# Projections of a streaming encoder: one pass over the channel tiles for both token groups, instead of one pass for each

## The chip, the cores and the metric
The kernel runs on one core of one Trainium2 chip. The metric is device time in microseconds (us) of one execution; a profile is taken of one execution, and its times count from the start of its span.

## The reference
Two layers of a hybrid streaming encoder are computed for 512 prompt frames, 16 meta tokens and 32 new frames of a sample stream, 560 tokens of 1024 channels in all. What matters here is that nearly all of the arithmetic is dense projections:

```python
h = _rmsnorm(x, p['g_pre_mix'])
... = _split_cols(h @ p['w_in'])          # queries, keys, values, three branch gates
y = (g[..., 0, :] * (oa @ p['w_up_a']) + g[..., 1, :] * (ob @ p['w_up_b'])
     + g[..., 2, :] * (oc @ p['w_up_c']))
x = x + _rmsnorm(y @ p['w_out'], p['g_post_mix'])
f = jnp.square(jax.nn.relu(_rmsnorm(x, p['g_pre_mlp']) @ p['w_ff1'])) @ p['w_ff2']
```

Branch A is latent attention, B is sliding-window attention, C is a gated linear recurrence (GLA).

## The kernel before
**Units.** Tokens lie along the free axis, channels on the 128 partitions. The weights of a layer are cut into 151 units of 128 x 1024 values, each with a kind and a number: `kralr`, `cq`, `ck`, `cv`, `cg`, `ckv` (branch C and latents), `qr`, `qn`, `qb`, `kb`, `vb`, `gate_a/b/c`, `up_a/b/c`, `out`, `ff1`, `ff2`. A unit makes 128 output channels from 8 channel tiles, or (`up_a`, `up_b`) two sets of 128 output channels from 4 channel tiles each.

**Token groups.** The 560 tokens are two halves of 280 (`H[0]`, `H[1]`), because one PSUM bank takes one half. Each float32 operand is held as a rounded high part and a low part (`hi_w`, `lo_w` of the weights, `hi_x`, `lo_x` of the tokens), and a product is three matmuls, called records here: high by high, low weight by high, high weight by low. A half of a unit is therefore 24 records into one bank, a whole unit 48.

**Order.** A plan written by hand (`layer_plan`, `lap`) gives the order of steps, the same for every engine. A step `("dense", u)` is a whole unit, `("half", u, hf)` one half of it; between them stand the steps of the three branches (`gla`, `att`, `prep_a`, `b`). `dense_unit` issues a unit on TensorE. Near the turn from one layer part to the next, halves are issued apart; there are 117 whole units a layer, and one of them (`out` 0) has a branch of its own in `dense_unit`.

**Banks.** Six PSUM banks serve the units, given out at build time to the half whose turn it is, least recently used first, out of a set that depends on the unit:

```python
b = 5 if key in guests else min(SIX if wide else FOUR if ... else THREE if ... else TWO, key=lambda c: bank_free[c])
```

`out`, `ff1` and `ff2` take from six banks. Units from `qb` 1 to the last `up_b` take from three. Nearly all others, those of the GLA and attention stretches, take from two, because attention and the recurrence hold the rest. `wait_bank` makes TensorE wait until the bank's previous half has been evacuated.

**Evacuation.** ScalarE (ACT) evacuates `ck`, `cg`, `vb`, `out`, `ff1`; VectorE (DVE) the rest, half 0 and then half 1, in the order of the plan. A gate's half goes through both: on ACT an absolute value (L1386), an exponential (L1387) and a logarithm (L1388), then on DVE the step that frees the bank (L1785), then on ACT a last exponential (L1390); only then does ACT turn to the other half. GpSimd (POOL) computes the low parts of weights and scales attention probabilities.

Of the kernel before, what the change touches and what calls it, by code (L numbers as in the profile page):

```python
# [88 lines left out]
def outs_of(kind):  # L89

    return (2, 4) if kind in ("up_a", "up_b") else (1, KD)
# [51 lines left out]
def build(nc, io, known):  # L143
    st = Steps(known)
    ctx = ExitStack()
    with ctx:
        def sem(name):
            return ctx.enter_context(nc.semaphore(name))
# [159 lines left out]
        pe_done, act_done, dve_done, pool_done = (sem(n) for n in ("pe_done", "act_done", "dve_done", "pool_done"))  # L308
# [63 lines left out]
        for i, m in enumerate((1, 2, 4, 8, 16)):  # L372
            a = 2 * 128 + i * (META + DEC) // 2
# [13 lines left out]
        def program(block):  # L387
            H = (slice(0, HALF), slice(HALF, T))

            def A(e, n, layer=None):  # L390
                return st.at(e, n, st.layer if layer is None else layer)
# [5 lines left out]
            def source(kind, n):  # L397
                if kind == "up_c":
                    return "oc"
                if kind == "up_a":  # L400
                    return "oa"
                if kind == "up_b":
                    return "ob"
                if kind == "out":
                    return "y"
                if kind == "ff1":
                    return "h2"
                if kind == "ff2":
                    return "hid%d" % (n // 8 % 2)
                return "h"  # L410

            def ready_names(kind, n, k):

                s = source(kind, n)
                if s == "ob":
                    return ("act", "ob hi 4"), ("pool", "ob lo 4")
                if s.startswith("hid"):
                    g = n // 8
                    return ("act", f"hid hi {8 * g + k}"), ("pool", f"hid lo {8 * g + k}")
                lo = y_engine_of_lo(k) if s == "y" else "dve" if s == "oc" else "pool"  # L420
                return ("act", f"{s} hi {k}"), (lo, f"{s} lo {k}")

            def y_engine_of_lo(k):
                return "dve" if k >= 6 else "pool"

            def evac_engine(kind):
                return "act" if kind in ("ck", "cg", "out", "ff1", "vb") else "dve"
# [241 lines left out]
            for l_ in range(DEPTH):  # L669
                for u in range(NU):  # L670
                    kind, n = UNITS[u]
# [9 lines left out]
            for l_, step in plan:  # L681
# [15 lines left out]
                while begun and split and most:  # L697
                    key = split[0]
# [17 lines left out]
            for i, key in enumerate(halves):  # L716
                l_, u, o, hf = key
                kind = UNITS[u][0]
                wide = kind in ("out", "ff1", "ff2") or u in V_NEXT
                b = 5 if key in guests else min(SIX if wide else FOUR if UIDX["qn", 2] <= u <= UIDX["up_c", 0] else THREE if UIDX["qb", 1] <= u < UIDX["out", 0] else TWO, key=lambda c: bank_free[c])  # L720
# [10 lines left out]
            def low_split(u):  # L731
                return (dve_done, A("dve", f"w lo {u}")) if (st.layer, u) in on_dve else (pool_done, A("pool", f"w lo {u}"))

            def bank(u, o, hf):
                return bank_of[st.layer, u, o, hf]
# [9 lines left out]
            by_name = {"pe": pe_done, "act": act_done, "dve": dve_done, "pool": pool_done}  # L745
# [133 lines left out]
            def _(pe):  # L879
                first_use = set()  # L880

                def wait_bank(u, o, hf):
                    prev = before[l, u, o, hf]
                    if (l, u, o, hf) in guests:
                        i = guests[l, u, o, hf]
                        pe.wait_ge(dve_done, A("dve", f"b o {i - 1}" if i > 0 else f"a o {len(jobs) - 1}"))
                    if prev is not None:
                        pl, pu, po, ph = prev
                        e = evac_engine(UNITS[pu][0])
                        pe.wait_ge(by_name[e], A(e, f"evac {pu} {po} {ph}", pl))  # L890

                def dense_unit(u, hfs):
                    kind, n = UNITS[u]
                    nout, kt = outs_of(kind)
                    slot = slot_of[l, u]
                    hi_w = whi[slot][:, :].rearrange("p (k m) -> p k m", k=kt)
                    lo_w = wlo[slot][:, :].rearrange("p (k m) -> p k m", k=kt)
                    src = source(kind, n)
                    hi_x, lo_x = moving[src]
                    halved = src in ("h", "h2")  # L900
                    pe.wait_ge(act_done, A("act", f"w hi {u}"))
                    pe.wait_ge(*low_split(u))
                    if kind == "qn" and n == 2:
                        pe.wait_ge(act_done, A("act", f"gla rstd {C_HEADS - 1}"))
                    if kind == "out" and n == 0:
                        pe.wait_ge(dve_done, A("dve", "b o 4"))
                    m = 112 if kind == "kralr" else 128
                    if src == "y" and n == 0:

                        for hf in range(2):  # L910
                            wait_bank(u, 0, hf)
                        for k in range(kt):
                            for e, name in ready_names(kind, n, k):
                                pe.wait_ge(by_name[e], A(e, name))
                            for hf in range(2):
                                for i, (a, b) in enumerate(((hi_w, hi_x), (lo_w, hi_x), (hi_w, lo_x))):
                                    mm = pe.matmul(bank(u, 0, hf)[0:m, :], a[:, k, 0:m], b[:, k, H[hf]],
                                                   start=(k == 0 and i == 0), stop=(k == kt - 1 and i == 2))
                                if k == kt - 1:
                                    mm.then_inc(pe_done, st.done("pe", f"half {u} 0 {hf}"))  # L920
                        st.mark("pe", f"dense {u}")
                        return
                    for o in range(nout):
                        for hf in hfs:
                            wait_bank(u, o, hf)
                            key = (l, src, n // 8 if kind == "ff2" else 0, hf if halved else 0)
                            fresh = key not in first_use
                            first_use.add(key)
                            for k in range(kt):
                                if fresh and halved:  # L930
                                    which, at_l = ("next", l - 1) if src == "h" else ("pre_mlp", l)
                                    pe.wait_ge(act_done, A("act", f"{which} hi {k} {hf}", at_l))
                                    pe.wait_ge(dve_done, A("dve", f"{which} lo {k} {hf}", at_l))
                                elif fresh:
                                    for e, name in ready_names(kind, n, k):
                                        pe.wait_ge(by_name[e], A(e, name))
                                for i, (a, b) in enumerate(((hi_w, hi_x), (lo_w, hi_x), (hi_w, lo_x))):
                                    mm = pe.matmul(bank(u, o, hf)[0:m, :], a[:, k, o * 128:o * 128 + m], b[:, k, H[hf]],  # L938
                                                   start=(k == 0 and i == 0), stop=(k == kt - 1 and i == 2))
                            mm.then_inc(pe_done, st.done("pe", f"half {u} {o} {hf}"))  # L940
                    if hfs[-1] == 1:
                        st.mark("pe", f"dense {u}")
# [376 lines left out]
                for l, step in order:  # L1319
# [22 lines left out]
                    elif step[0] == "att":  # L1342
                        br, j = step[1], step[2]
                        n = len(JOBS[br])
# [1232 lines left out]
```

## Time and profile before

| | us |
|---|---|
| median of 3 runs | 2324.94 (2324.63 to 2325.22) |
| the profiled execution's own time | 2323.95 |
| its span | 2322.2 |
| TensorE matmul busy | 2283.4 (98%) |
| VectorE, ScalarE, GpSimd busy | 915.2, 995.9, 934.7 |

The profiled execution is 1 us under the median, and 1.75 us of its time lie around the span. In the rows below, `PE` is TensorE's matmuls and `PEld` its weight loads; a row of a timeline has the start, the duration, the engine, the line, the operation, the tile written and those read, and in brackets the idle time before it with what ended that. Durations of matmuls overlap: how fast they follow each other is read from their starts. `dense<-` are records into banks 0 and 1, `att<-` records into the other banks.

### The profile page before, as it was taken

What the parts mean: (1) busy time and instruction counts of PE and PEld (TensorE: products, weight loads), DVE (VectorE), ACT (ScalarE), POOL (GpSimd) and SP (SyncE); (2) the same over time, 40 slices, a digit from 0 to 9 for tenths busy, and PEclk for the clock granted to TensorE, in tenths of its full rate; (3) what the DMA queues carried; (4) which work ended last, traced back from release to release, by engine and by line L of the source; (5) the groups of instructions that cost most, each with busy time, mean ns of one, the idle gap of its engine ahead of it and who ended that gap; (6) DMA issues with size and microseconds to landing.
All of it is one profiled execution on the core that took longest, in us unless ns stands there. A gap on an engine that the chain in (4) does not pass through costs nothing.

```text
span 2322.2 us, 41257 instructions
## 1 busy us (share of the span) xinstructions
PE 2283.4 (98%) x17472; PEld 2167.5 (93%) x17472; DVE 915.2 (39%) x1909; ACT 995.9 (43%) x1879; POOL 934.7 (40%) x600
## 2 busy tenths in 40 slices
PE   7999999999999999999999999999999999999997
PEld 7999978889899999999999999788999999999997
DVE  6566555544514401001575664555344153000014
ACT  4444334443555642332344444344345556433412
POOL 2222224444665453544412222144455645545432
PEclk9999999999999999999999999999999999999999
DMA  5121221122124222222321222211212241222222
GB/s 193 54 65 62 84 78 58 55 63 73 63 82 154 69 82 91 83 85 71 118 88 53 72 62 88 68 61 56 72 65 65 82 167 55 83 91 82 89 80 72
DMA packets 59815, 187.89 MB, mean 81 GB/s; under 512 B 8400, under 2 KB 17552, under 8 KB 59120
## 3 DMA queue, kind: packets, MB, share of 16 engines
q1 hardware_dynamic: 51408, 169.28, 23.1%
q10 hardware_dynamic: 8224, 15.97, 1.9%
q8 instruction: 139, 2.28, 0.4%
q14 instruction: 44, 0.36, 0.0%
HBM read 170.99 MB, written 10.89 MB: 78 GB/s over the span
## 4 chain that ended last, share of the span: by engine, by line
PE 92%; DVE 5%; ACT 1%; issue 1%; POOL 0%; DMA 0%; SPq 0%; DVEq 0%; ACTq 0%
PE dense L938 44%; PE att L938 30%; PE att L1013 2%; PE att L1242 1%; PE att L1153 1%; PE att L1090 1%; PE att L1173 1%; PE att L1280 1%; PE dense L967 1%; PE att L1094 1%; PE att L1076 1%; PE att L1315 1%; PE att L1201 1%; PE att L1177 1%; DVE x L1879 1%
## 5 line engine op out<-in xcount | busy, mean ns | idle before, releaser
L2299 POOL TENSOR_TENSOR wlo<-wraw,whi 128x1024 fp32r<-128x1024 f32 x245 | 588.4, 2409 | 596.8 <-ACT whi L1367 596.8
L938 PE MATMUL dense<-h_hi,whi 128*128 128x280 f32 x1888 | 557.4, 295 | 1.2 <-issue 0.9
L938 PE MATMUL dense<-h_lo,whi 128*128 128x280 f32 x1888 | 551.0, 292 | 0.0
L938 PE MATMUL dense<-h_hi,wlo 128*128 128x280 f32 x1888 | 549.9, 291 | 0.0
L1367 ACT ACTIVATE whi<-wraw 128x1024 fp32r<-128x1024 f32 x302 | 315.0, 1050 | 267.9 <-DMA wraw<-in_w 265.2
L938 PEld LDWEIGHTS dense<-h_hi,whi 128*128 128x128 f32 x1888 | 355.6, 188 | 14.5 <-issue 11.1
L938 PEld LDWEIGHTS dense<-h_hi,wlo 128*128 128x128 f32 x1888 | 355.1, 188 | 0.5
L938 PEld LDWEIGHTS dense<-h_lo,whi 128*128 128x128 f32 x1888 | 355.4, 188 | 0.0
L938 PE MATMUL att<-h_hi,whi 128*128 128x280 f32 x1024 | 299.3, 292 | 0.4 <-issue 0.4
L938 PE MATMUL att<-h_lo,whi 128*128 128x280 f32 x1024 | 298.3, 291 | 0.0
L938 PE MATMUL att<-h_hi,wlo 128*128 128x280 f32 x1024 | 297.8, 291 | 0.0
L938 PE MATMUL att<-hid_hi,whi 128*128 128x280 f32 x672 | 196.0, 292 | 0.0
L938 PEld LDWEIGHTS att<-h_hi,whi 128*128 128x128 f32 x1024 | 192.4, 188 | 3.5 <-ACT sig L1390 1.6
L938 PE MATMUL att<-hid_lo,whi 128*128 128x280 f32 x672 | 195.6, 291 | 0.0
L938 PE MATMUL att<-hid_hi,wlo 128*128 128x280 f32 x672 | 195.3, 291 | 0.0
L938 PEld LDWEIGHTS att<-h_hi,wlo 128*128 128x128 f32 x1024 | 192.2, 188 | 0.3
L938 PEld LDWEIGHTS att<-h_lo,whi 128*128 128x128 f32 x1024 | 192.4, 188 | 0.0
L2304 POOL TENSOR_TENSOR hid_lo<-hid_raw,hid_hi 128x560 fp32r<-128x560 f32 (+1 forms) x76 | 93.6, 1231 | 239.0 <-ACT hid_hi L1371 239.0
L2347 POOL TENSOR_TENSOR level<-bcum 128x256 f32<-128x256 f32 (+2 forms) x56 | 42.8, 764 | 262.6 <-DVE bcum L1928 262.6
L938 PEld LDWEIGHTS att<-hid_hi,whi 128*128 128x128 f32 x672 | 126.3, 188 | 0.1
L938 PEld LDWEIGHTS att<-hid_lo,whi 128*128 128x128 f32 x672 | 126.3, 188 | 0.0
L938 PEld LDWEIGHTS att<-hid_hi,wlo 128*128 128x128 f32 x672 | 126.2, 188 | 0.1
(366 smaller groups left out, 4581.2 us busy)
## 6 DMA issues: line engine op xcount, KB each, us to landing
wraw<-in_w SPq DMA_DIRECT2D x302, 512.0 KB, 3.5
x_spill<-x ACTq DMA_DIRECT2D x2, 2240.0 KB, 7.0
x<-x_spill ACTq DMA_DIRECT2D x2, 2240.0 KB, 11.9
k_cat<-k_rope SPq DMA_DIRECT2D x16, 212.0 KB, 3.4
x<-in_x SPq DMA_DIRECT2D x4, 560.0 KB, 6.0
out_y_out<-x SPq DMA_DIRECT2D x4, 560.0 KB, 3.1
out_c_out<-ckv SPq DMA_DIRECT2D x2, 560.0 KB, 5.4
state<-in_state ACTq DMA_DIRECT2D x8, 128.0 KB, 2.1
```

Source lines behind the costliest of these rows:

```text
L938: mm = pe.matmul(bank(u, o, hf)[0:m, :], a[:, k, o * 128:o * 128 + m], b[:, k, H[hf]], start=(k == 0 and i == 0), stop=(k == kt - 1 and i ...
L967: mm = pe.matmul(bank(u, 0, hf)[0:m, :], a[:, k, 0:m], b[:, k, H[hf]], start=(k == 0 and i == 0), stop=(k == KD - 1 and i == 2))
L1013: mm = pe.matmul(ps[0:rows, PAIR_BANK[i], c0:c0 + 64].rearrange("p (g t) -> p g t", t=m), e[:, 128 * sb:128 * sb + rows], late, start=(n_ ...
L1076: mm = pe.matmul(ps[:, bank, 256 * (sb % 2):256 * (sb % 2) + 256], ktok[0:n, sb, :], vtok[0:n, sb, :], start=(sb % 2 == 0), stop=True, ski ...
L1090: pe.matmul(dst, vtok[0:n, sb, 128 * vt:128 * vt + 128], amat[0:n, a:a + n], start=first, stop=(sb == 0), skip_group_check=True)
L1094: mm = pe.matmul(dst, state[:, STATE_IN[sb], 128 * vt:128 * vt + 128], qe[:, a:a + n], start=False, stop=True, skip_group_check=True)
L1153: mm = pe.matmul(ps[0:n, pair + i, 0:512], src[:, k, a:a + n], wuv[:, k, :], start=(k == 0), stop=(k == KL - 1))
L1173: mm = pe.matmul(ps[:, S0 + a, 0:META + 128 * (i + 1)], q_cat[:, h, 128 * i:128 * i + 128], k_cat[:, h, K_META:K_FRAME + 128 * (i + 1)], s ...
L1367: act.activation(whi[slot][:, :], wraw[slot][:, :], ACT.Copy).then_inc(act_done, st.done("act", f"w hi {u}"))
L2299: pool.tensor_tensor(wlo[slot][:, :], wraw[slot][:, :], whi[slot][:, :].bitcast(F32), ALU.subtract).then_inc(pool_done, st.done("pool", f" ...
L2304: pool.tensor_tensor(lo, raw, hi.bitcast(F32), ALU.subtract).then_inc(pool_done, st.done("pool", name))
L2347: pool.tensor_tensor(e_first, ref, b_first, ALU.subtract).then_inc(pool_done, st.done("pool"))
```

## The change
A branch is added to `dense_unit` for calls with both halves. For each set of output channels it first waits for the banks of both halves, then goes through the channel tiles once. For each tile it issues six records: high weight by high half 0 and half 1, high weight by low half 0 and half 1, low weight by high half 0 and half 1. So four records with the same stationary tile stand in a row, then two, and the bank changes at each record. Halves that are issued apart (`("half", ...)`, `("pair", ...)`) and `out` 0 are as before, and so are the bank of each half, the plan and the order on every other engine.

```diff
--- before.py
+++ after.py
@@ -920,6 +920,25 @@
                                     mm.then_inc(pe_done, st.done("pe", f"half {u} 0 {hf}"))
                         st.mark("pe", f"dense {u}")
                         return
+                    if len(hfs) == 2:
+                        for o in range(nout):
+                            for hf in hfs:
+                                wait_bank(u, o, hf)
+                            key = (l, src, n // 8 if kind == "ff2" else 0, 0)
+                            fresh = key not in first_use
+                            first_use.add(key)
+                            for k in range(kt):
+                                if fresh:
+                                    for e, name in ready_names(kind, n, k):
+                                        pe.wait_ge(by_name[e], A(e, name))
+                                for i, (a, b, hf) in enumerate(((hi_w, hi_x, 0), (hi_w, hi_x, 1), (hi_w, lo_x, 0), (hi_w, lo_x, 1),
+                                                                (lo_w, hi_x, 0), (lo_w, hi_x, 1))):
+                                    mm = pe.matmul(bank(u, o, hf)[0:m, :], a[:, k, o * 128:o * 128 + m], b[:, k, H[hf]],
+                                                   start=(k == 0 and i < 2), stop=(k == kt - 1 and i >= 4))
+                                    if k == kt - 1 and i >= 4:
+                                        mm.then_inc(pe_done, st.done("pe", f"half {u} {o} {hf}"))
+                        st.mark("pe", f"dense {u}")
+                        return
                     for o in range(nout):
                         for hf in hfs:
                             wait_bank(u, o, hf)
```

TensorE, inside unit `gate_b` 0 of layer 0, before: the end of half 0 (bank 1, `dense`) and the start of half 1 (bank 4, `att`), where the wait for that bank's evacuation stands.

```order
L938 MATMUL dense<-h_hi,whi_77 128x280
L938 MATMUL dense<-h_hi,wlo_64 128x280
L938 MATMUL dense<-h_lo,whi_77 128x280
L938 MATMUL att<-h_hi,whi_77 128x280 [waits dve_done]
L938 MATMUL att<-h_hi,wlo_64 128x280
L938 MATMUL att<-h_lo,whi_77 128x280
```

TensorE, the end of the same unit and the start of `gate_b` 1 (banks 0 and 1) now.

```order
L936 MATMUL dense<-h_hi,whi_77 128x280
L936 MATMUL att<-h_hi,whi_77 128x280
L936 MATMUL dense<-h_lo,whi_77 128x280
L936 MATMUL att<-h_lo,whi_77 128x280
L936 MATMUL dense<-h_hi,wlo_64 128x280
L936 MATMUL att<-h_hi,wlo_64 128x280
L936 MATMUL dense<-h_hi,whi_75 128x280 [waits dve_done,pool_done,act_done]
```

The two halves end side by side, and the wait for both banks of the next unit stands ahead of its first record.

TensorE, where `gate_b` 1 (banks 0 and 1, here `dense0` and `dense1`) ends and `up_b` 0 begins, before; `up_b` 0 takes banks 4 and 0 for its first output channels.

```order
L938 MATMUL dense1<-h_lo_89,whi0_75 128x280
L938 MATMUL dense1<-h_hi_90,whi0_75 128x280
L938 MATMUL dense1<-h_hi_90,wlo0_62 128x280
L938 MATMUL dense1<-h_lo_89,whi0_75 128x280
L938 MATMUL att<-ob_hi_155,whi1_76 128x280 [waits act_done,dve_done,pool_done]
L938 MATMUL att<-ob_hi_155,wlo1_63 128x280
L938 MATMUL att<-ob_lo_154,whi1_76 128x280
```

The same place now.

```order
L936 MATMUL dense0<-h_hi_90,wlo0_62 128x280
L936 MATMUL dense1<-h_hi_90,wlo0_62 128x280
L936 MATMUL att<-ob_hi_155,whi1_76 128x280 [waits dve_done,act_done,pool_done]
L936 MATMUL dense0<-ob_hi_155,whi1_76 128x280
L936 MATMUL att<-ob_lo_154,whi1_76 128x280
L936 MATMUL dense0<-ob_lo_154,whi1_76 128x280
L936 MATMUL att<-ob_hi_155,wlo1_63 128x280
L936 MATMUL dense0<-ob_hi_155,wlo1_63 128x280
```

Bank 0 was last written 24 records before `up_b` 0 and is needed 12 records into it; now it is written until two records ahead of it and needed at once.

## Rows read from the trace of the kernel before

**Rows 1.** Page: busy us, share of the span, instructions.
```profile
PE 2283.4 (98%) x17472; PEld 2167.5 (93%) x17472; DVE 915.2 (39%) x1909; ACT 995.9 (43%) x1879; POOL 934.7 (40%) x600
```

**Rows 2.** Page: chain that ended last, share of the span by engine.
```profile
PE 92%; DVE 5%; ACT 1%; issue 1%; POOL 0%; DMA 0%; SPq 0%; DVEq 0%; ACTq 0%
```

**Rows 3.** Windows: us, then busy us (count) by engine, granted clock, DMA share, GB/s.
```profile
634.00:709.00 75.00, 75.00 (x585) 74.63 (x583) 13.92 (x33) 43.32 (x83) 47.69 (x28) 1.00 0.28 86
802.00:1123.00 321.00, 321.00 (x2502) 321.00 (x2501) 22.82 (x51) 107.64 (x159) 158.05 (x80) 1.00 0.28 86
```

**Rows 4.** TensorE's waits: who waited for whom, total us, times, longest.
```profile
PE att L981 <- DVE nsum L1856: 15.3, 5, 10.8
...
PE att L1280 <- DVE qb L1816: 1.5, 2, 0.7
```

**Rows 5.** Line L1100: durations of loads and records, two calls with one stationary each time.
```profile
L1100 PEld LDWEIGHTS att<-gsq,const x32: 189/189/190, 120.8 to 1438.1; 128*128 128x128 f32 x32
L1100 PE MATMUL att<-gsq,const x32: 398/398/399, 121.0 to 1438.4; 128*128 128x280 f32 x32
```

**Rows 6.** Timeline, ff1 and ff2 units: start us, us, engine, line, operation.
```profile
833.41 0.41 ACT L1426 ACTIVATE hid_raw<-att 128x280 f32<-128x280 f32 x1 [2.69 <-PE att L938]
...
870.20 0.29 PE L938 MATMUL att<-hid_hi,whi 128*128 128x280 f32 x1
...
870.40 0.45 DVE L1831 COPY facc<-att 128x280 f32<-128x280 f32 x1 [2.62 <-PE att L938]
```

**Rows 7.** Timeline around the end of gate_c 2, all engines.
```profile
375.20 1.02 PE L1177 MATMUL att<-k_cat,q_cat 128*128 128x512 f32 x2
...
375.40 0.40 ACT L1386 ACTIVATE sig<-dense 128x280 f32<-128x280 f32 x1 [0.66 <-PE dense L938]
...
376.85 0.45 DVE L1785 SCALAR_TENSOR_TENSOR sig<-dense,sig 128x280 f32<-128x280 f32 x1 [2.58 <-ACT sig L1388]
...
377.33 0.44 ACT L1390 ACTIVATE sig<-sig 128x280 f32<-128x280 f32 x1 [0.58 <-DVE sig L1785]
...
377.53 0.17 DVE L2112 MEMSET att<- 64x128 f32 x1 [0.24 <-PE att L1178]
...
379.55 0.39 PE L938 MATMUL dense<-oc_hi,whi 128*128 128x280 f32 x1
```

**Rows 8.** Timeline, TensorE after gate_c 1 and after gate_a 1.
```profile
358.29 1.08 PE L1173 MATMUL att<-k_cat,q_cat 128*128 128x272 f32 x4
...
359.86 0.37 PE L938 MATMUL dense<-oc_hi,whi 128*128 128x280 f32 x1
...
500.97 0.29 PE L938 MATMUL dense<-h_lo,whi 128*128 128x280 f32 x1
501.49 1.09 PE L1201 MATMUL att<-const,prob 128*128 128x128 f32 x8 [0.22 <-POOL prob L2373]
...
502.44 0.38 PE L938 MATMUL dense<-h_hi,whi 128*128 128x280 f32 x1
```

**Rows 9.** Timeline: probabilities of attention job 3, and TensorE's use of them.
```profile
384.22 1.95 POOL L2373 TENSOR_TENSOR prob<-prob,stat 128x1056 f32<-128x1056 f32 x1 [3.06 <-DVE stat L2190]
...
387.07 1.09 PE L1201 MATMUL att<-const,prob 128*128 128x128 f32 x8
```

**Rows 10.** Timeline in the preparation of the keys, after gate_c 0.
```profile
334.40 0.17 DVE L2084 COPY k_cat<-att 64x16 f32<-64x16 f32 x1
...
334.62 0.53 PEld L1147 LDWEIGHTS att<-cct,wuk 128*128 128x128 f32 x3 [0.51 <-DVE k_cat L2084]
```

**Rows 11.** Timeline, TensorE between two units of the GLA stretch.
```profile
173.21 1.10 PE L1100 MATMUL att<-gsq,const 128*128 128x280 f32 x4
173.94 0.50 PE L938 MATMUL dense<-h_hi,whi 128*128 128x280 f32 x1
```

**Rows 12.** Windows around one wait in each layer; columns as in rows 3.
```profile
772.00:784.00 12.00, 9.61 (x59) 8.97 (x58) 10.33 (x18) 8.43 (x19) 2.90 (x3) 0.86 0.00 1
1921.00:1933.00 12.00, 9.63 (x72) 8.99 (x70) 10.33 (x18) 8.60 (x20) 2.91 (x3) 1.00 0.01 1
```

## The prediction
> **What bounds the kernel now.** The page comes first: matmuls are busy for 2283.4 us, 98% of the span [rows 1], and 92% of the chain that ended last runs through TensorE [rows 2]. So the question for every edit is whether TensorE's stream of records gets shorter, or gets holes. Next, the windows. In the last projections of a layer (634 to 709 us) and in the MLP (802 to 1123 us) TensorE is busy for the whole stretch; there 2502 records take 321 us, one each 0.128 us [rows 3]. A whole unit of 48 records takes 6.16 us. Then TensorE's waits: the longest group is 15.3 us, and 1.5 us in two places is already the fourth [rows 4]. No group of waits for a bank is in that list. The evacuations are hidden entirely, and what hides them is the order: while a half is evacuated, the other half of the same unit is computed, 24 records or 3.08 us.
>
> **What the change does to the records.** Of 117 whole units a layer 116 take the new branch: 232 units, 11,136 records. None is removed or added. Is a record cheaper when its stationary tile is the one before? The nearest rows are those of L1100, where two calls in a row have the same constant as stationary tile: 32 records, and 32 weight loads of 189 ns [rows 5]. Each record brings its load all the same. So the load of a repeated tile stays, and I take the spacing as it is, 0.128 us: the cycle of today already mixes records that share the moving tile with the one before and records that share nothing, and the mean is 0.128 over all [rows 3]. Bounds: an effect of the repeated tile, or of the alternating bank, is in no row. Records of L1100 with 280 columns and full precision show the slow end, four in 1.10 us with 0.40 us for one, so 0.23 us apart [rows 5, 11]; 0.02 us less than now would be a sixth, and I keep 0.02 us either way as bounds, 7,424 to 11,136 records times 0.02, up to 223 us. The value is nearest to zero because the dense records themselves, in whatever order their operands repeat, are the nearest rows.
>
> The Trainium skill speaks for a gain here: in "TensorE: Matmul & The Clock Gate", Part 2 ("What happens when you issue a matmul"), it says that weights stay put across many matmuls, so that one loads once and multiplies repeatedly. The rows above show a load with each record, so by them that saving isn't made in this program; by the rule it is the first rival below.
>
> **What it does to the banks.** Before, half 0 was complete 24 records ahead of the unit's end; now both halves end together. Everything that evacuated half 0 under half 1 moves behind the unit. If the next user of a bank follows at once, TensorE waits. I count time from E, the moment when the next record would start. Prices, from rows:
> - DVE, plain: the next record starts at 870.20, the copy at 870.40 and takes 0.45 [rows 6], so the bank is free at E + 0.65. ACT, plain: the same with 0.41 [rows 6], E + 0.61.
> - A gate: E is 375.20; ACT starts at 375.40, DVE ends at 376.85 + 0.45 = 377.30, the last exponential at 377.77 [rows 7]. So E + 2.10 for one half. Now half 0 is E + 2.10 less 0.13 (its last record is one earlier), its last exponential ends at E + 2.44, and half 1 takes another 1.90 from there: E + 4.4.
> - When a semaphore lets TensorE go on it starts 0.06 later: DVE ends at 334.57, the load starts at 334.62 [rows 10].
>
> So a wait is 2.05 for a gate's half 0, 0.6 for a plain half 0, 1.0 for two plain halves, 4.4 for a gate's two halves, less the other TensorE work that stands between. By stretch, for one layer:
> - Last projections, four groups of two gates and one `up_b` on three banks, nothing between. The second gate needs the bank of the first one's half 0: 2.05. `up_b` needs the bank of the second one's half 0: 2.05. Its second output channels need the first half of its first: 0.6. The next gate needs the half after: 0.6, in three of four. 8 x 2.05 + 7 x 0.6 = 20.6. The second halves come free well before they are needed.
> - Attention, two banks, units alternately `gate` and `up_c`, with attention's matmuls between. After `gate_c` 1 those last from 358.29 to 359.86, 1.57; after `gate_a` 1 from 501.10 (the start of the last record and 0.13) to 502.44, 1.34 [rows 8]. Waits 4.4 - 1.57 = 2.8 and 3.05. After the other gates they last 4.35, as after `gate_c` 2 [rows 7], or 3.96, read likewise: no wait, or 0.45 in three places. But DVE also begins the softmax of the next job only when it has freed half 1: at 377.53 now [rows 7], E + 2.33, and at E + 4.38 then, 2.05 later. The probabilities of job 3 are ready at 386.17, TensorE takes them up at 387.07 [rows 9]: 0.9 of slack, 1.15 lost, in three places. Those of job 15 are waited for already [rows 8]: 2.0 lost. Sum 2.8 + 3.05 + 1.35 + 3.45 + 2.0 = 12.65.
> - Keys: after `gate_c` 0 DVE copies keys for which TensorE waits already, 0.05 after the copy [rows 10]; DVE comes 2.2 later. `qn` has two copies a half, 4 x 0.45 and 0.1 = 1.95 after E; 0.73 of matmuls of the kind in [rows 11] stand between: 1.25. The rotation behind it, without slack, loses 0.75. Sum 4.2.
> - GLA, read in the same way from unit to unit: mostly 2.5 to 7 us of its matmuls stand between units; after `ckv` 1 nothing (1.0), in two places 0.73 [rows 11] (0.3 each), in one 0.2. Sum 1.8.
> - Before branch B: `vb` to `qb` 0 1.0, two `qb` 0.6 each, and 0.3 more of a wait that exists [rows 4]. Sum 2.5.
> - MLP: six banks, so a bank is needed again two units, 12 us, after its unit's end. Nothing. ACT there has 107.6 us of work in 321 [rows 3], which covers the shift; without it each unit would pay 1.0.
>
> Per layer 41.75, both layers 83.5. A record after a wait is followed 0.1 later than 0.13 (the row at 379.55 is 0.39 long where 0.29 is usual, [rows 7]); 19 new places a layer make 3.8. Sum 87.
>
> A seventh term is the clock. Each layer has a stretch of 12 us in which TensorE idles for 2.4 us, mostly in one wait. In the one the granted clock was 0.86, so it stood for 3.4 us at the lower of its two levels (1.2 instead of 2.4 GHz), and 59 records were done where the other did 72 at a clock of 1.00 [rows 12]: 13 records, 1.7 us. So an idle of that size costs it once in two. The new waits of 2 us and more, 12 a layer, are a little shorter; I take one in six, 4 x 1.7 = 7. Bounds none and all, 0 and 41.
>
> Against the profiled execution: 2323.95 + 87 + 7 = 2418, and as that is 1 under the median, **2419 us** against 2324.94. Waits are packed twice at a unit's start instead of once at each half; a unit's start shows no gap today with two or three waits there, so I cost that at nothing.
>
> **Rivals.**
> 1. *Records get cheaper and win* (the other side). If a repeated tile made its record faster, the waits would be paid back: 94 / 11,136 = 0.0084 us a record over all, or 0.0127 over the 7,424 that repeat a tile, decides the sign. At 0.02 us over the latter it is 148 saved: 2419 - 148 = 2271. For it: no row has four float32r records on one tile. Against it: [rows 5]. Chance 0.05; a part of it, a net 2340 to 2380, 0.08.
> 2. *The clock falls at each long wait.* The seventh term with every wait in it: 24 x 1.7 = 41 instead of 7, so 2452. For it: [rows 12]. Against it: the same idle time left the clock alone in the other layer, and most new waits are shorter. Chance 0.12.
> 3. *The waits are shorter*, since ACT and DVE catch up elsewhere, or the softmax isn't late: the attention and key terms away, 2 x 17: 2385. Chance 0.08. Nothing at all (2325), 0.02: only if the banks were free at once, which [rows 7] exclude.
>
> The Trainium skill has a rule for the second: "TensorE: Matmul & The Clock Gate", section "A second HAM failure mode: psum-queue depth-cycling", says that cycling through PSUM's queue lets TensorE idle briefly and the clock swing between its levels. This trace agrees that the lower level can follow an idle of about 2 us [rows 12].
>
> **Numbers.** The forecast, 2419 with a range of its own from 2400 to 2440, has 0.61; beside the rivals' 0.35, 0.04 is left for more than 2460. The range from 2383 to 2448 takes in the shorter waits and some of the clock's case. Under 0.2% (4.6 us) two measurements of this kernel can't be told apart. Faster 0.05, same 0.02, slower 0.93.
>
> **What would show it.** Right: dense records still 0.128 apart, as many loads as records; the MLP stretch still 321 us; the stretch of 75 us some 20 us longer, with new waits of TensorE for DVE's gate step (L1785, shifted by the new lines) of about 2 us, eight a layer; a list of waits that grows by some 80 us. Wrong: another spacing in the MLP, where banks play no part, would put rival 1 in its place; a granted clock under 1.00 in the last projections, rival 2; a stretch from 344 to 517 that grows by much more than 13, a knock-on through the softmax that I have undercounted.

## The result, and the profile after

The changed kernel takes 2440.4 us (median of 4 runs, 2437.3 to 2443.8) where the kernel before took 2324.8: a ratio of 1.0498, 95% interval 1.0485 to 1.051, or 115.6 us more. The forecast was 2419, the range 2383 to 2448. The profiled execution took 2441.9 us, 1.5 above the median, and the one before was 0.8 under its own; so the spans below differ by 118.0 us, more than the medians. Lines behind L941 have moved by 19: the gate's step on DVE is L1804 now, the branch's records are L936.

The page first: busy time by engine, then the shares of the chain that ended last by engine.

```profile
PE 2327.0 (95%) x17472; PEld 2200.0 (90%) x17472; DVE 912.3 (37%) x1909; ACT 982.5 (40%) x1879; POOL 934.9 (38%) x600
...
PE 86%; DVE 7%; ACT 4%; issue 2%; POOL 1%; DMA 0%; DVEq 0%; ACTq 0%; SPq 0%
```

Against [rows 1, 2]: every record still brings its load (17472 and 17472), TensorE has fallen from 98% to 95% of a longer span, and what it lost in the chain went for the most part to DVE and ACT, the engines that evacuate. Its busy time has grown by 44 us although no record was added; part of that is a lower clock, as the windows show. First the last projections of either layer, then the MLP (columns as in rows 3):

```profile
657.70:768.40 110.70, 90.92 (x586) 87.59 (x583) 13.30 (x32) 42.30 (x83) 49.63 (x28) 0.88 0.19 58
1866.20:1973.80 107.60, 87.83 (x585) 84.52 (x583) 13.26 (x32) 42.32 (x83) 48.47 (x28) 0.90 0.19 59
861.30:1184.20 322.90, 322.90 (x2502) 322.90 (x2501) 20.09 (x51) 104.18 (x158) 158.01 (x80) 1.00 0.27 86
```

The stretch that took 75.00 us, all busy, at a clock of 1.00 [rows 3] takes 110.70 and 107.60, is idle for 20 us, and has a clock of 0.88 and 0.90. The MLP takes 322.90 us for the 2502 records that took 321.00, without any idle time. TensorE's waits (who for whom, total us, times, longest):

```profile
PE dense L936 <- DVE sig L1804: 28.3, 19, 2.6
PE att L1000 <- DVE nsum L1875: 15.3, 5, 10.8
PE att L936 <- DVE sig L1804: 12.5, 6, 2.2
PE att L1220 <- POOL prob L2392: 12.1, 8, 2.4
PE dense L936 <- DVE sig L1844: 5.0, 10, 0.5
...
PE att L1166 <- DVE k_cat L2103: 4.4, 2, 2.2
PE att L1159 <- DVE rtmp L2061: 4.2, 2, 2.1
```

Only the second line stood at the head of the list before [rows 4]. Two groups wait for the gate's step on DVE, 25 times, and one, eight times, for attention's probabilities; L1844 is the plain evacuation of `up_b`. The first of these waits in the last projections, TensorE, ACT and DVE in the order of time, with ACT's steps in between left out (gate_b 0 ends, gate_b 1 begins):

```profile
664.41 0.29 PE L936 MATMUL att<-h_hi,wlo 128*128 128x280 f32 x1
664.67 0.41 ACT L1405 ACTIVATE sig<-dense 128x280 f32<-128x280 f32 x1 [5.52 <-PE dense L936]
...
666.11 0.45 DVE L1804 SCALAR_TENSOR_TENSOR sig<-dense,sig 128x280 f32<-128x280 f32 x1 [7.36 <-ACT sig L1407]
666.71 0.50 PE L936 MATMUL dense<-h_hi,whi 128*128 128x280 f32 x2 [2.01 <-DVE sig L1804]
666.94 0.39 ACT L1405 ACTIVATE sig<-att 128x280 f32<-128x280 f32 x1
...
668.37 0.45 DVE L1804 SCALAR_TENSOR_TENSOR sig<-att,sig 128x280 f32<-128x280 f32 x1 [1.80 <-ACT sig L1407]
```

This is [rows 7] with its cover gone. ACT and DVE need the same times as before, but ACT had been idle for 5.52 us and DVE for 7.36: both got all their work at the unit's end. From the start of the last record to that of the next one it is 2.30 us, 2.17 more than usual. In windows of the same place, the wait and then two stretches behind it:

```profile
664.40:666.70 2.30, 0.30 (x3) 0.10 (x2) 0.45 (x1) 1.38 (x4) 0.00 (x0) 1.00 0.36 61
...
667.70:671.10 3.40, 3.40 (x17) 3.40 (x16) 0.45 (x1) 1.92 (x4) 0.79 (x1) 0.50 0.01 2
671.10:674.40 3.30, 3.30 (x28) 3.30 (x26) 0.00 (x0) 0.00 (x0) 1.61 (x1) 1.00 0.00 0
```

The clock is 1.00 while TensorE waits. It falls to 0.50 a microsecond after TensorE has gone on, and stays there for 3.4 us, full of records: 17, where 28 follow in the next 3.30 us. So the wait's own time hides none of it here.

By stretch, from the end of one unit to the end of another in both traces (growth in us; forecasts without the 1.9 a layer for restarts and the 7 for the clock):

| stretch | forecast | layer 0 | layer 1 |
|---|---|---|---|
| GLA and keys, to `up_c` 0 | 6.0 | 8.25 | 8.11 |
| attention | 12.65 | 12.18 | 11.38 |
| before branch B | 2.5 | 2.50 | 2.52 |
| branch B | 0 | 0.27 | 0.23 |
| last projections | 20.6 | 35.74 | 32.30 |
| `out` and the turn to the MLP | 0 | -0.16 | 0.45 |
| MLP | 0 | 1.87 | 1.85 |

That is 117.5 us; another 0.5 lies ahead of the first whole unit, and the spans differ by 118.0.

### The profile page after: what moved, and what is told of

It reads as the page before. It is cut to its first block, busy times and chain, and to the rows that moved or that the text cites. A ratio compares the mean times of both kernels' runs of the same rounds, so it can differ in the third digit from the quotient of the medians.

```text
span 2440.2 us, 41495 instructions
## 1 busy us (share of the span) xinstructions
PE 2327.0 (95%) x17472; PEld 2200.0 (90%) x17472; DVE 912.3 (37%) x1909; ACT 982.5 (40%) x1879; POOL 934.9 (38%) x600
## 4 chain that ended last, share of the span: by engine, by line
PE 86%; DVE 7%; ACT 4%; issue 2%; POOL 1%; DMA 0%; DVEq 0%; ACTq 0%; SPq 0%
PE dense L936 36%; PE att L936 21%; PE att L957 8%; PE dense L957 5%; PE att L1032 2%; PE att L1172 1%; PE att L1109 1%; PE att L1095 1%; ACT sig L1406 1%; ACT sig L1407 1%; PE dense L986 1%; PE att L1299 1%; DVE sig L1804 1%; ACT sig L1405 1%; PE att L1113 1%
## 5 line engine op out<-in xcount | busy, mean ns | idle before, releaser
L936 PE MATMUL dense<-h_hi,whi 128*128 128x280 f32 x1728 | 406.7, 299 | 23.3 <-DVE sig L1804 12.7
L936 PE MATMUL dense<-h_hi,wlo 128*128 128x280 f32 x1728 | 397.2, 293 | 0.0
L936 PE MATMUL dense<-h_lo,whi 128*128 128x280 f32 x1728 | 396.8, 293 | 0.0
L936 PEld LDWEIGHTS dense<-h_hi,whi 128*128 128x128 f32 x1728 | 288.1, 190 | 38.7 <-issue 16.6
L936 PEld LDWEIGHTS dense<-h_hi,wlo 128*128 128x128 f32 x1728 | 288.9, 190 | 0.0
L936 PEld LDWEIGHTS dense<-h_lo,whi 128*128 128x128 f32 x1728 | 288.5, 190 | 0.0
L936 PE MATMUL att<-h_hi,whi 128*128 128x280 f32 x736 | 188.7, 295 | 5.0 <-DVE sig L1804 4.0
L936 PE MATMUL att<-h_hi,wlo 128*128 128x280 f32 x736 | 187.8, 294 | 0.0
L936 PE MATMUL att<-h_lo,whi 128*128 128x280 f32 x736 | 187.1, 293 | 0.0
L936 PE MATMUL att<-hid_hi,wlo 128*128 128x280 f32 x544 | 138.3, 292 | 0.0
L936 PE MATMUL att<-hid_hi,whi 128*128 128x280 f32 x544 | 137.9, 292 | 0.0
L936 PE MATMUL att<-hid_lo,whi 128*128 128x280 f32 x544 | 137.5, 291 | 0.0
L936 PEld LDWEIGHTS att<-h_hi,whi 128*128 128x128 f32 x736 | 129.9, 190 | 6.3 <-ACT sig L1407 4.4
L936 PEld LDWEIGHTS att<-h_hi,wlo 128*128 128x128 f32 x736 | 129.8, 190 | 0.0
L936 PEld LDWEIGHTS att<-h_lo,whi 128*128 128x128 f32 x736 | 129.4, 190 | 0.0
L1804 DVE SCALAR_TENSOR_TENSOR sig<-dense,sig 128x280 f32<-128x280 f32 x70 | 31.5, 450 | 241.8 <-ACT sig L1407 240.0
L936 PEld LDWEIGHTS att<-hid_hi,whi 128*128 128x128 f32 x544 | 95.0, 188 | 0.0
```

The lines of the kernel that those rows point to most:

```text
L1804: ins = dve.scalar_tensor_tensor(s, src, 0.0, s, ALU.min, ALU.subtract)
```

## The experiments

### The MLP alone, and the order of its records
The new branch for `ff1` and `ff2` alone, where six banks leave no wait (the code in this section is cut to the lines that change; `...` marks what is left out):

```diff
-                    if len(hfs) == 2:
+                    if len(hfs) == 2 and kind in ("ff1", "ff2"):
```

> The new branch for ff1 and ff2 alone (52 units a layer, six banks). Theory (the change costs waits for banks, and the clock that falls in them; a record costs what it did): nothing waits here, so it keeps only the growth of the MLP stretch in the trace of the changed kernel, 1.85 us a layer, 3.7 in all: 2324.8 + 3.7 = 2328.5 us, with no lower clock. Rival (a repeated stationary tile makes its record cheaper, and the waits hide that): 104 units of 32 repeating records at 0.0084 us or more each, 28 us or more, so under 2297. Rival (the branch costs by the unit, wherever it runs): 104 of 232 units, 104/232 of 115.6 us = 52, so 2377.

Measured: 2328.56 us, ratio 1.0014 (1.0005 to 1.0023). The MLP of layer 0:

```profile
802.90:1125.80 322.90, 322.90 (x2502) 322.90 (x2501) 20.13 (x51) 104.17 (x158) 157.94 (x80) 1.00 0.27 86
```

So 104 of the 232 units cost 3.7 us together: the loss doesn't come by the unit, and no gain is hidden under it.

The kernel before, halves apart, with the high tile twice in a row:

```diff
-                                for i, (a, b) in enumerate(((hi_w, hi_x), (lo_w, hi_x), (hi_w, lo_x))):
+                                for i, (a, b) in enumerate(((hi_w, hi_x), (hi_w, lo_x), (lo_w, hi_x))):
```

> The kernel before, with its halves apart, but high by high, high by low, low by high: the high stationary tile twice in a row, no alternating banks, no new waits. Theory (each record loads its tile all the same): 2324.8 us, within 2; 17472 loads, spacing in the MLP 0.128 us. Rival (a repeated tile is cheaper): some 3700 records repeat a tile, at 0.0127 us each 47 us less, 2278.

Measured: 2325.17 us, ratio 0.9999 (0.999 to 1.0008); the MLP is as long as in [rows 3]:

```profile
802.80:1123.80 321.00, 321.00 (x2502) 321.00 (x2501) 22.82 (x51) 107.50 (x159) 157.84 (x80) 1.00 0.27 86
```

A repeated tile gains nothing by itself. Then one pass for `ff1` and `ff2` alone, banks alternating, but with one repeat in six records where there were four (the order of the six, as weight, tokens and half):

```diff
-  (hi_w, hi_x, 0), (hi_w, hi_x, 1), (hi_w, lo_x, 0), (hi_w, lo_x, 1), (lo_w, hi_x, 0), (lo_w, hi_x, 1)
+  (hi_w, hi_x, 0), (lo_w, hi_x, 1), (hi_w, lo_x, 0), (hi_w, hi_x, 1), (lo_w, hi_x, 0), (hi_w, lo_x, 1)
```

> As the MLP run, ff1 and ff2 alone in one pass, banks alternating at each record, but with tiles in the order high, low, high, high, low, high, so that one record in six repeats a tile instead of four. If the 3.7 us of the MLP come from the alternating banks: 2328.5 us, as with four repeats. If they come from the repeated tiles: a quarter of it, 2325.7. If repeats were cheaper and alternating dearer: above 2328.5.

Measured: 2328.71 us, ratio 1.0015 (1.0006 to 1.0024), the stretch again 322.90 us for 2502 records:

```profile
801.90:1124.80 322.90, 322.90 (x2502) 322.90 (x2501) 20.11 (x50) 104.18 (x158) 157.93 (x80) 1.00 0.27 86
```

Last of these, again `ff1` and `ff2` alone, three records into one bank and then three into the other:

```diff
+  (hi_w, hi_x, 0), (lo_w, hi_x, 0), (hi_w, lo_x, 0), (hi_w, hi_x, 1), (lo_w, hi_x, 1), (hi_w, lo_x, 1)
```

> ff1 and ff2 in one pass as in the MLP run, but three records into one bank, then three into the other (high by high, low by high, high by low for half 0, then for half 1): the bank changes at every third record. The MLP stretch grew by 1.85 us a layer with a change at each record, whichever tiles repeat. If the change of bank costs, it grows by a third, 0.6 us a layer, 2326.3 in all; if it is the passing of both halves over one channel tile, by 1.85 again, 2328.6.

Measured: 2326.23 us, ratio 1.0006 (0.9997 to 1.0015). The time alone can't tell this from no change, but the stretch can, 0.7 us longer instead of 1.9:

```profile
802.40:1124.10 321.70, 321.70 (x2502) 321.70 (x2501) 21.03 (x51) 106.60 (x158) 158.08 (x80) 1.00 0.28 86
```

What costs is the change from one half to the other, some 0.75 ns each time (1.85 us by 2496 changes; with a third of the changes 0.7 us), whichever tiles repeat. Bank and moving half change together in all of these, so which of the two it is stays open.

### All but the last projections

```diff
-                    if len(hfs) == 2:
+                    if len(hfs) == 2 and kind not in ("gate_b", "up_b"):
```

> The new branch for all but gate_b and up_b (the last projections, 24 of 232 units, go back to two passes). Theory: the growth of that stretch goes, 35.75 us in layer 0 and 32.31 in layer 1: 2440.4 - 68.1 = 2372.3 us, and the lower clock is gone there. Rival (cost by the unit): 24/232 of 115.6 = 12, so 2428.

Measured: 2374.88 us, ratio 1.0214 (1.02 to 1.0228). The stretch is back at the 75.00 us of [rows 3]:

```profile
657.30:732.30 75.00, 75.00 (x585) 74.65 (x583) 13.93 (x33) 43.28 (x83) 47.67 (x28) 1.00 0.29 86
```

A tenth of the units has 57% of the loss (65.5 of 115.6 us).

### Filling the waits: what the clock takes

```diff
+                FILLED = [UIDX["gate_b", n] for n in (1, 3, 5, 7)] + [UIDX["up_b", n] for n in (0, 2, 4, 6)]
...
                     if len(hfs) == 2:
+                        if u in FILLED:
+                            for i in range(12):
+                                pe.matmul(ps[0:m, T0, 0:HALF], hi_w[:, 0, 0:m], moving["h"][0][:, 0, H[i % 2]], start=True, stop=True)
```

> The changed kernel with 12 further records (1.54 us) into a bank that nothing reads, ahead of each of the eight waits of 2.17 us in a layer's last projections; they leave the waits' ends where they are. Theory (13.4 and 10.3 us of the growth there are the clock, which falls because TensorE idles): the clock stays at 1.00 in that stretch, and 2440.4 - 23.7 = 2416.7 us. Rival (the clock falls for another reason, or its fall costs nothing because the time is waited anyway): 2440. Rival (the records lie on the path): 16 x 1.54 = 24.6 more, 2465.

Measured: 2418.99 us, ratio 1.0408 (1.0391 to 1.0425), 21 less than the changed kernel with 192 records more. The first filled wait (L928 are the added records), and the two stretches:

```profile
661.14 0.29 PE L941 MATMUL att<-h_hi,wlo 128*128 128x280 f32 x1
661.27 1.71 PE L928 MATMUL att<-h_hi,whi 128*128 128x280 f32 x12
663.44 0.50 PE L941 MATMUL dense<-h_hi,whi 128*128 128x280 f32 x2 [0.47 <-DVE sig L1809]
```

```profile
654.50:752.70 98.20, 91.02 (x679) 87.75 (x678) 13.23 (x32) 42.39 (x83) 48.42 (x28) 1.00 0.22 66
1852.60:1950.90 98.30, 91.35 (x682) 87.80 (x679) 13.30 (x32) 42.38 (x83) 48.52 (x28) 1.00 0.21 65
```

The next unit starts 2.30 us after the last record of the one before, to the hundredth as in the changed kernel: the wait for the bank is as long. But TensorE is idle for 0.47 us of it instead of 2.01, and the clock is 1.00 throughout. The stretch grows by 23.39 and 22.97 us instead of 35.74 and 32.30. The difference, 21.7 us, is what idling cost there through the clock; what is left is the waits and the records' small extra time.

### Gates in two passes, the rest in one

```diff
-                    if len(hfs) == 2:
+                    if len(hfs) == 2 and not kind.startswith("gate"):
```

> The new branch for all but the gates (gate_a, gate_b, gate_c go back to two passes; their evacuation goes through ACT, DVE and ACT). Theory: it is the gates' long evacuation behind the unit that is waited for. In the last projections one wait of 0.67 is left of each group of four, 2.7 us a layer instead of 35.75 and 32.31; in attention the waits after the two gates with little work behind them become 0.5 and 0.75 and the softmax starts as early as before, so some 10.5 of 12 a layer go; of the keys' 3.05 some 1.5: 2440.4 - 62.7 - 21 - 3 = 2354 us, and no lower clock in the last projections. Rival (any unit whose halves end together costs the same): gates are 24 of 116 units a layer, 24 us less, 2416.

Measured: 2355.22 us, ratio 1.0128 (1.0113 to 1.0143). TensorE's waits in the attention stretch of layer 0, and the last projections:

```profile
PE dense L936 <- DVE sig L1804: 1.1, 2, 0.7
PE att L1220 <- POOL prob L2392: 0.2, 1, 0.2
```

```profile
643.60:721.70 78.10, 76.09 (x586) 74.91 (x583) 13.31 (x32) 43.28 (x83) 48.60 (x28) 1.00 0.26 82
```

Attention grows by 1.71 us instead of 12.18, with the two bank waits of 0.4 and 0.7, and the softmax is as early as before. The last projections grow by 3.1 instead of 35.74. `up_b` and `up_c` are still in one pass, so the 85 us that this gives back are the gates': it is the evacuation through ACT, DVE and ACT that must have another half to hide under. Part of the 85 is the clock, which fell behind the gates' waits.

### Attention: bank or softmax

```diff
-                    if len(hfs) == 2:
+                    if len(hfs) == 2 and kind not in ("up_c", "kb"):
```

> The changed kernel with up_c and kb, the units behind the gates of the attention stretch, in two passes again; the gates stay in one. Their first half then needs the bank of the gate's half 0 alone, free at E + 2.1 in place of E + 4.4; DVE still begins the softmax 2.05 later. Theory (two causes in attention: banks 7.2 and late softmax 5.45 of the forecast 12.65): the bank part falls from 7.2 to 0.5 + 0.75, the softmax part stays: some 5.9 us less a layer, 2440.4 - 12 = 2428.5 us, the stretch about 6 longer than before. Rival (only the late softmax): 2440, the stretch 11 to 12 longer as now. Rival (only the banks): about 2419, the stretch 1 to 2 longer.

Measured: 2433.14 us, ratio 1.0469 (1.0452 to 1.0487); attention grows by 6.83 us in either layer. TensorE's waits in that stretch of layer 0, here and then in the changed kernel:

```profile
PE att L1220 <- POOL prob L2392: 6.2, 4, 2.4
PE dense L957 <- DVE sig L1804: 0.4, 1, 0.4
```

```profile
PE att L1220 <- POOL prob L2392: 6.1, 4, 2.4
PE dense L936 <- DVE sig L1804: 3.8, 4, 2.6
```

The banks' part goes and the softmax's stays. Both causes are there, the late softmax being the larger one. The total came out 4.6 us above its forecast. Attention gave back 5.35 and 4.55 us instead of 5.9 a layer; the 0.8 between them is a fall of the clock that the changed kernel's profile has in layer 0. The rest has no one place: branch B grew by 1.80 and 1.76 instead of 0.27 and 0.23, with a fall in either layer that the profile of the changed kernel doesn't have, while the last projections had 12 falls instead of 14 and came out 3.6 us shorter. Falls vary from one execution to the next.

### Six banks, and what is late next
Once branch B is done, three more banks are idle. The changed kernel, with all six for the last projections (the added wait holds TensorE until DVE has done the last step of branch B):

```diff
-  min(SIX if wide else FOUR if ...
+  min(SIX if wide or UIDX["gate_b", 1] <= u < UIDX["out", 0] else FOUR if ...
...
+                        if (kind, n) == ("gate_b", 1):
+                            pe.wait_ge(dve_done, A("dve", "b o 4"))
```

> The changed kernel with six banks instead of three for the last projections (from gate_b 1 on; three of them are idle there once branch B is done). Theory (the waits there are for banks, and the clock falls in the waits): neither is left: 2440.4 - 68.1 = 2372 us, a stretch of 68 us again. Rival (the alternating banks or the order of tiles cost there themselves): less than half of that back, 2406 or more.

Measured: 2395.89 us, ratio 1.0305 (1.029 to 1.0321). Only 44.5 of the 68 us come back, so the theory as stated fell short. In each layer four waits of 2.06 to 2.42 us were left, all ahead of an `up_b`. The second of them, ACT, GpSimd and TensorE:

```profile
690.47 1.04 ACT L1388 ACTIVATE whi<-wraw 128x1024 fp32r<-128x1024 f32 x1
...
691.59 2.35 POOL L2320 TENSOR_TENSOR wlo<-wraw,whi 128x1024 fp32r<-128x1024 f32 x1 [4.42 <-ACT whi L1388]
...
691.85 0.29 PE L938 MATMUL dense<-h_hi,wlo 128*128 128x280 f32 x1
...
694.04 0.37 PE L938 MATMUL dense<-ob_hi,whi 128*128 128x280 f32 x1 [1.90 <-ACT sig L1409]
```

The row puts TensorE's wait down to ACT's L1409, which no bank of `up_b` needs. What does end there is the low part of `up_b`'s weights on GpSimd, 691.59 + 2.35 = 693.94. It is late because ACT makes the high part (690.47) only behind both halves of the gate two units ahead. The next run moves the weight steps ahead of that evacuation:

```diff
+            for l_ in range(DEPTH):
+                for u_ in range(UIDX["up_b", 0], UIDX["out", 0]):
+                    full.remove((l_, ("w", u_)))
+                    full.insert(full.index((l_, ("dense", u_ - 2))), (l_, ("w", u_)))
```

> The six-bank run came out at 2395.9 us: in each group the wait of 2.06 ahead of up_b stayed, four a layer, one of which takes the clock along (stretch 10.4 us longer than before in either layer). There GpSimd's low part of up_b's weights lands last (691.59 and 2.35 make 693.94; TensorE goes on at 694.04): ACT makes the high part only behind the gate's evacuation. Now the weight step of each unit of the last projections stands ahead of the evacuation of the unit two before it, not behind it. Theory (late weights are what is left): 8 x 2.06 and 2 x 1.7 back, 2395.9 - 20 = 2376 us, clock 1.00 in the stretch. Rival (up_b waits for a bank or for its tokens all the same): 2396.

Measured: 2384.43 us, ratio 1.0256 (1.0241 to 1.0271), 11.5 of the 20 us that were expected. The stretch was as short as before (0.3 us longer in layer 0, 0.1 shorter in layer 1), but a wait of 2.02 us had come up at `out` 0, whose weight step had not been moved (GpSimd, then TensorE):

```profile
734.05 5.20 POOL L2324 TENSOR_TENSOR wlo<-wraw,whi 128x1024 fp32r<-128x1024 f32 x2 [8.43 <-ACT whi L1392]
...
736.51 0.37 PE L921 MATMUL att<-oc_hi,whi 128*128 128x280 f32 x1 [1.85 <-issue]
```

So that one too, the range reaching to `UIDX["out", 0] + 1`:

> In the run before the stretch of the last projections was as short as in the kernel before (0.3 us longer), but out 0 came to wait 2.02 us in either layer, and the clock fell with it: GpSimd's low part of its weights starts at 734.05, behind two gates' evacuation on ACT, and TensorE goes on at 736.51. Now the weight step of out 0 stands earlier too. Theory (one late weight after the other): 2 x 3.6 us back, 2384.4 - 7.2 = 2377 us. Rival (the wait moves on to the next unit again): 2384.

Measured: 2375.0 us, ratio 1.0214 (1.0199 to 1.0229), the same as without one pass in this stretch at all.

```profile
657.60:732.80 75.20, 75.20 (x584) 74.84 (x583) 12.89 (x32) 42.52 (x83) 47.87 (x28) 1.00 0.28 85
```

And the earlier weights with the three banks of the changed kernel:

> The changed kernel (three banks) with the weight steps of the last projections that much earlier. Theory (with three banks the wait ahead of up_b ends with the bank, and the weights are ready some 0.3 us earlier): nothing, 2440 us, within 3 for the clock. Rival (the waits of 2.17 there were for weights): half of them go, 2 x 4 x 2.17 and as many falls of the clock at 1.7, 31 less, 2409.

Measured: 2442.24 us, ratio 1.0506 (1.0489 to 1.0524): nothing, and the 15 gaps in the last projections add up to 22.2 us as without it. There the bank is later than the weights; in the kernel before both were on time.

None of these versions is faster than the kernel before. Where there are banks enough the one pass costs 0.5 to 0.75 ns a record (0.27 us for 576 records in the last projections of layer 0 with six banks and both weights early, 1.85 us for 2496 in the MLP), where there aren't it costs waits, and nowhere does it give anything back.

## Why the prediction was right, and where it was off

The direction and the mechanism were right: both halves end together, the evacuation comes out from under the other half, and TensorE waits for banks, for the softmax and for the keys. The time lies in the range, 21 us above the forecast and just past the forecast's own 2400 to 2440, and one term makes up most of that. Two of the signs that the prediction named against itself came in part: the clock under 1.00 in the last projections, its rival 2, and another spacing in the MLP, 0.129 us, though on the slower side and so not its rival 1.

**The clock was mis-sized: 7 forecast, 25 measured.** The step was "I take one in six, 4 x 1.7 = 7". In the changed kernel's trace the granted clock is at 0.50 for 3.4 us 19 times (one more lies at the end of the span in both kernels); before, once, in the turn to the MLP [rows 12]. Summed over the records in those stretches, what their spacing exceeds 0.128 us by is 26.7 us, against 1.6 before: about 1.5 to 1.6 for a fall among dense records, near the 1.7 of the forecast. It is the frequency that was wrong: 14 of the 16 gate waits in the last projections were followed by a fall, and 3 of the other 8 long ones (2.1 to 2.6 us); the remaining 2 are in the turns to the MLP. Rival 2 had all 24; the truth lies nearer to it than to the forecast. The filled waits show the cause apart from the waiting: same waits, clock 1.00, 21.7 us back. How often it falls can't be read from the length of a wait alone: the longest, 2.62 us after `gate_c` 1, was followed by a fall in neither layer, and with six banks 2 of 8 waits of 2.06 to 2.42 us were. Why 2 of 8 there and 14 of 16 here is open. The Trainium skill, "TensorE: Matmul & The Clock Gate", section "A second HAM failure mode: psum-queue depth-cycling", has bursts between brief idle times pay for the clock's return; these stretches agree, with a clock of 0.88 and 0.90.

**The waits were right in sum: 87 forecast, about 85 left** (118.0 us of span less 25 for the clock and an estimated 8 for the records). In the last projections the 15 gaps add up to 22.2 us in either layer; the working had 20.6 and 15 x 0.1 for the restarts, 22.1.
- In attention [rows 7 to 9] the parts came as forecast: 2.62 for 2.8 after `gate_c` 1, 0.38 three times for 0.45, 1.2 three times for 1.15, 2.41 in all for job 15, where 0.22 was waited before. The step that failed is the 3.05 after `gate_a` 1: it was added to the 2.0 of job 15, but TensorE stands in that very wait while the bank comes free. In layer 1, 0.69 us of it is left behind job 15's 2.41. In layer 0 nothing is, because the clock stood at 0.50 from 520.9 on and the eight records of job 15 took 1.79 us instead of 1.09. So the waits of attention add up to 10.4 us in layer 1 (6.1 for the probabilities and 4.5 for the gate's step, less 0.2 waited before), 2.2 less than forecast; this and the rotation below partly offset each other, and the sum agrees better than its parts. The rows, first after `gate_c` 1 and of job 3, then after `gate_a` 1 in layer 0 and in layer 1:

```profile
371.49 0.49 PE L936 MATMUL dense<-oc_hi,whi 128*128 128x280 f32 x2 [2.62 <-DVE sig L1804]
...
400.07 1.09 PE L1220 MATMUL att<-const,prob 128*128 128x128 f32 x8 [1.23 <-POOL prob L2392]
...
520.70 1.79 PE L1220 MATMUL att<-const,prob 128*128 128x128 f32 x8 [2.41 <-POOL prob L2392]
...
522.60 0.81 PE L936 MATMUL dense<-h_hi,whi 128*128 128x280 f32 x2
...
1730.00 1.09 PE L1220 MATMUL att<-const,prob 128*128 128x128 f32 x8 [2.41 <-POOL prob L2392]
...
1731.90 0.50 PE L936 MATMUL dense<-h_hi,whi 128*128 128x280 f32 x2 [0.69 <-DVE sig L1804]
```

- GLA and keys grew by 8.2 instead of 6.0. The keys' 2.2 [rows 10] is there to the digit (4.4 in two layers, L1166 in the list of waits); the rotation loses 1.6 a layer (4.2 in all, 0.5 a layer before), not 0.75; some 1.0 is the records' term, 28 units of 48 at the MLP's rate.
- Before branch B 2.5 was forecast and 2.50 and 2.52 came. In the MLP no wait was forecast and none came.

**The records' term was 0 and is some 5 to 8.** Within its bounds of 0.02 us a record, but not nothing: 0.75 ns for each record that changes halves, 1.85 us a layer measured in the MLP, and at the same rate some 8 us for 11,136 records. That is an estimate: in the last projections with six banks the rate was 0.5 ns, by which it would be 5 (and the waits 88). Rival 1 is excluded: with one repeat in three records and no alternation the time is that of before, and with alternation four repeats in six take as long as one. The Trainium skill, "TensorE: Matmul & The Clock Gate", Part 2 ("What happens when you issue a matmul"), has weights loaded once and multiplied repeatedly; the trace doesn't show that here, where the number of loads stays 17472 with the repeats, and the MLP without alternation stays at 321.00 us.

Two late things were not in the working because the bank waits hid them: the weights of `up_b` and of `out` 0. They cost nothing in the changed kernel. With six banks the first cost 10 us a layer in the last projections, and once it was early the second cost 9.4 in all.

## What to carry to other kernels

Computing one half while the other is evacuated is double buffering, even where no line says so: before merging two passes, set the time from a bank's last record to its release against the work that then stands ahead of the bank's next user, place by place, and count a wait that stands behind another wait only for what is left of it. Price a wait of 2 us of TensorE in a dense stretch at the wait and the records that a lower clock loses behind it, 1.5 us here, since it may come nearly each time. When a wait is removed, look for the operand that was ready only because of it; here it was weights, twice.

## What the runs showed of the hardware

- The clock fell behind the waits, not in them: in the last projections the lower level (0.50) began 2.2 to 3.6 us after the start of the last record ahead of a wait that ended after 2.3 to 2.5, and so nearly its whole length hit records. Records put into the waits, whose results nothing uses, made the changed kernel 21 us faster.
- Four records on one stationary tile are no faster than records on changing ones, and records that alternate between halves are 0.75 ns slower each in the MLP; its whole units took some 1.9 us more (322.90 for 321.00) with either order that alternates at each record.
